# Expert routing lists built on chip and spread over the last mixer block, in one program block instead of four

## The reference, cut to what matters

```
lg  = h2 @ w_rg + b_rg                 # 4 groups, the best one is taken
le  = h2 @ w_re + b_re                 # 32 experts, top 2 of the 8 in that group
gate = softmax(top 2) * softmax(lg)[group]
# each (token, expert) pair is given a slot in a block that one expert owns
hid = silu(x[block] @ w_gate[e]) * (x[block] @ w_up[e])
y[token] += (hid @ w_down[e]) * gate
out = rmsnorm(x + y, g_final)
```

## Time and profile before

| | us |
|---|---|
| median of 3 runs (1652.87 to 1655.18) | 1653.35 |
| profiled execution: its own time | 1655.35 |
| profiled execution: span, first to last instruction | 1653.70 |
| PE busy | 1497.3 (91%) |
| DVE busy | 1035.1 (63%) |
| ACT busy | 867.5 (52%) |
| POOL busy | 340.5 (21%) |

### The profile page before, as it was taken

The page is one execution under the profiler, slowest core; times in us unless marked ns, Lnnn a source line. Parts: engine busy times, 40 slices in busy tenths (PEclk is TensorE's granted clock), DMA queues, the critical chain, the costliest instruction groups (busy, mean ns, idle before and its releaser), DMA issues. The chain is left out here.

```text
span 1653.7 us, 24203 instructions
## 1 busy us (share of the span) xinstructions
PE 1497.3 (91%) x8174; PEld 1250.7 (76%) x8174; DVE 1035.1 (63%) x1491; ACT 867.5 (52%) x1177; POOL 340.5 (21%) x486
## 2 busy tenths in 40 slices
PE   6999999999999999999999606999999999999980
PEld 5888899988889998888999604767666666666650
DVE  4565444656444546654453326899888888888853
ACT  4644433464444336544432214777777777777742
POOL 1122111111111111212110041222222223222213
PEclk9999999999999999999999757999999999999995
DMA  6222533342234435223332138999999999999956
GB/s 226 77 80 95 189 115 117 117 162 77 90 128 153 129 101 179 77 89 116 115 127 96 77 115 319 376 381 371 380 373 378 379 371 380 375 379 378 372 185 238
DMA packets 71504, 350.77 MB, mean 212 GB/s; under 512 B 10705, under 2 KB 10978, under 8 KB 46706
## 3 DMA queue, kind: packets, MB, share of 16 engines
q1 hardware_dynamic: 57554, 310.05, 50.6%
q0 software_dynamic: 9824, 25.28, 6.6%
q10 hardware_dynamic: 4048, 14.42, 2.3%
HBM read 322.42 MB, written 27.75 MB: 212 GB/s over the span
## 5 line engine op out<-in xcount | busy, mean ns | idle before, releaser
L1227 DVE TENSOR_TENSOR wlo<-est,whi 128x2048 fp32r<-128x2048 f32 x193 | 440.9, 2291 | 112.8 <-ACT whi L1223 85.4
L1223 ACT ACTIVATE whi<-est 128x2048 fp32r<-128x2048 f32 x193 | 369.3, 1916 | 151.4 <-DMA est<-wexp 115.9
L734 DVE TENSOR_TENSOR w<-stage,w 128x1024 fp32r<-128x1024 f32 x171 | 219.6, 1311 | 65.9 <-ACT w L483 64.0
L1582 PE MATMUL ps<-whi,xT 128*96 128x512 f32 x512 | 205.3, 401 | 24.7 <-DVE xT L1532 24.4
L483 ACT ACTIVATE w<-stage 128x1024 fp32r<-128x1024 f32 x171 | 174.3, 1052 | 101.2 <-PE ps L995 86.5
L1584 PE MATMUL ps<-whi,xT 128*96 128x512 f32 x512 | 203.3, 397 | 0.0
L1583 PE MATMUL ps<-wlo,xT 128*96 128x512 f32 x512 | 202.4, 395 | 0.0
L993 PE MATMUL ps<-w,hT 128*128 128x384 f32 x576 | 199.8, 347 | 0.0
L995 PE MATMUL ps<-w,hT 128*128 128x384 f32 x576 | 193.5, 336 | 0.0
L994 PE MATMUL ps<-w,hT 128*128 128x384 f32 x576 | 193.3, 336 | 0.0
L993 PE MATMUL ps<-hT,w 128*128 128x384 f32 x408 | 138.2, 339 | 4.7 <-DVE w L734 3.5
(11 more groups left out here) (221 smaller groups left out, 2681.0 us busy)
## 6 DMA issues: line engine op xcount, KB each, us to landing
est<-wexp SPq DMA_DIRECT2D x193, 1024.0 KB, 13.9
stage<-wmix SPq DMA_DIRECT2D x171, 512.0 KB, 3.6
H<-x_all SPq DMA_DIRECT2D x9, 512.0 KB, 8.2
XR<-x_all SPq DMA_DIRECT2D x9, 512.0 KB, 5.2
x_scratch<-XR ACTq DMA_DIRECT2D x9, 512.0 KB, 2.8
h_scratch<-H ACTq DMA_DIRECT2D x9, 512.0 KB, 5.0
cx<-x_scratch SPq DMA_DIRECT2D x9, 512.0 KB, 8.4
y_all<-co ACTq DMA_DIRECT2D x9, 512.0 KB, 6.7
```

Of the source, the lines that this page charges most:

```text
L734: vec.tensor_tensor(whl[w % 2][1][o], stage[r % STAGE][:], whl[w % 2][0][o].bitcast(F32), ALU.subtract).then_inc(w_lo, 1)
L1223: act.activation(whi[q][:], est[q][:], ACT.Copy).then_inc(e_hi[q], 1)
L1227: vec.tensor_tensor(wlo[q][:], est[q][:], whi[q][:].bitcast(F32), ALU.subtract).then_inc(e_lo[q], 1)
L1582: pe.matmul(out, A[0][ka], B[0][kb], start=start, stop=False)
```

## The change

The four program blocks become one, without the engines meeting between them. The list in DRAM goes (with its initial fill, the eighteen writes and all reads). Instead DVE makes, for each of 18 columns of pairs (nine tiles, two choices), a one-hot matrix `R` of the pair's slot within its block and a one-hot row `bk` of its block times the token's number, and PE adds up `R`-transposed times `bk`: the result, 96 slots by 32 experts, is the list. A second set of 18 such products (`bk2`) makes the gates and the lists of further blocks of experts with over 96 pairs. Each expert now always has a first block (block number = expert number), further blocks come behind block 31, and SP's loads ahead of the loop use the block number as the expert's. A slot without a pair gets index 2048; the gather has a bound and no error for it, and the scatter takes the spare row.

Ranking of the first six tiles (`rank_parts(0, 6)`, three parts) moves into the last group's z stage at d = 3, 4, 5; their rank products behind out product 2; their placement and the split of the first two weight pieces between the adds of column groups 1 and 2. Only the last three tiles are ranked behind the last logits. SP issues the last group's stores and, in its own order, loads for blocks 0, 1 and piece (2, 0) before the loop. In the loop POOL copies a column of the on-chip list into a 96x1 index tile twice a block (`gix`, `six`) in place of two list reads; DVE copies the gate column (`gwb`), which ACT's `y_out` waits for. Buffers are laid out anew: the tiles of pieces 0 and 1 lie where hT and oT were.

```diff
             def e_first(b, q):                       # SP, behind the last mixer weights
+                if b:
+                    sp.wait_ge(e_lo[q], b)
+                sp.dma_start(est[q][:], wexp[b, q]).then_inc(e_in[q], 16)
+            sp.wait_ge(br_mm, SUPER * DC)
+            for q in range(2):
+                e_first(0, q)
...
+            for j in range(TPS):
+                sp.wait_ge(n2_h, tot(last, TPS, j + 1))
+                sp.dma_start(h2_dram[...], H[j][:]).then_inc(h2_st[j], 16)
+                sp.dma_start(x2_dram[...], XR[j][:]).then_inc(x2_st[j], 16)
+            sp.wait_ge(out_mm, X2_OUT)
+            for q in (2, 3, 4):
+                e_first(0, q)
+            sp.wait_ge(log_mm, tot(last, TPS, TPS))
+            e_first(0, 5)
+            for b, q in ((1, 0), (1, 1), (1, 2), (1, 3), (2, 0)):
+                e_first(b, q)
+            sp.wait_ge(r_meta, 1)
...
+            hi(0, 0, True)                            # ACT, behind the out stage's splits
+            hi(0, 1, True)
+            square2(0, last)
+            square2(1, last)
+            act.wait_ge(w_lo, SUPER * NP_SB + SEED)
+            evac2(0)
+            square2(2, last)
+            evac2(1)
+            evac2(2)
...
+            def y_out(b):                             # ACT
+                act.wait_ge(e_used[5], b + 1)
+                act.wait_ge(gwb_cp, b + 1)
+                act.wait_ge(y_free, b + SEED)
+                act.activation(yS[:, 0:512], ps[0:TB, 5, :], ACT.Copy, scale=gwb[:]).then_inc(y_act, 1)
...
+            def gather(b, rows, first=False):         # POOL
+                if not first:
+                    pool.wait_ge(gx_tr, b)
+                pool.indirect_dma_start(out=gX[:], out_offset=None, in_=h2_dram,
+                                        in_offset=bass.IndirectOffsetOnAxis(ap=rows, axis=0),
+                                        bounds_check=ROWS - 1, oob_is_err=False).then_inc(gx_in, 16)
+            def gather_of(b):
+                pool.wait_ge(gx_in, b * 16)
+                pool.tensor_copy(gix[:], gidxf[:, bass.ds(b, 1)]).then_inc(gx_cp, 1)
+                pool.wait_ge(gx_cp, b - 2)
+                gather(b, gix[:])
+            def scatter(b):
+                pool.tensor_copy(six[:], sidx[:, bass.ds(b, 1)]).then_inc(six_cp, 1)
...
+            with pool.Fori(0, third_last) as b:
+                gather_of(b + 3)
+                scatter(b)
+                stored(b)
...
+            def place(part_, t0, nt, T):              # DVE
+                vec.wait_ge(r_rmm, part_ + 1)
+                link(vec.tensor_tensor(pick[:], oh[:], ranks..., ALU.mult))
+                link(vec.tensor_reduce(rk[:, i2], pick..., AX.X, ALU.add))
+                link(vec.tensor_tensor(cmp[:], rk..., steps..., ALU.is_ge))
+                link(vec.tensor_reduce(kq[:, i2], cmp[:], AX.X, ALU.add))
+                free(vec.scalar_tensor_tensor(key[:, i2], eid..., float(KEY), kq[:, i2], ALU.mult, ALU.add))
+                link(vec.scalar_tensor_tensor(slot[:, i2], kq[:, i2], -float(TB), rk[:, i2], ALU.mult, ALU.add))
+                free(vec.tensor_tensor(R[:, i2, :], cst3(C_SLOT, TB)..., slot..., ALU.is_equal))
+                link(vec.tensor_tensor(bk[:, i2, :], cst3(C_KEY, EXPERTS)..., key..., ALU.is_equal))
+                vec.tensor_tensor(b4, b4, tok, ALU.mult).then_inc(r_place, 1)
...
+            place(0, 0, EARLY, RA)                    # DVE, behind add_x2(1, 2)
+            lo(0, 0)
+            lo(0, 1)
+            add_x2(2, 0, last)
+            add_x2(2, 1, last)
+            norm2(0, last)
+            add_x2(2, 2, last)
+            norm2(1, last)
+            norm2(2, last)
             for j in range(TPS):
-                add_logits(j, SUPER - 1, j % 2, 0)
+                add_logits(j, last, 1, 0)
+            for _ in rank_parts(EARLY, TPS, RB):
+                pass
+            place(1, EARLY, TPS, RB)
+            vec.wait_ge(r_lmm, 1)
+            vec.tensor_scalar(gidx[:], lists, float(PAD_ROW), None, ALU.add).then_inc(r_list, 1)
...
+            x_lo(0)
+            lo(0, 2)
+            lo(0, 3)
+            pair_gates()
+            lo(1, 0)
+            body(0, first=True)
...
+            def list_mm(i0, i1):                      # PE
+                for i in range(i0, i1):
+                    ins = pe.matmul(ps[0:TB, B_LIST, 0:EXPERTS], R[:, i, :], bk[:, i, :], start=i == 0, stop=i == NP2 - 1)
...
+            route_logits(2, last, h2E[:, 2 * D:3 * D], 1, 0)
+            pe.wait_ge(r_place, 1)
+            list_mm(0, 2 * EARLY)
+            rank_mm(1, EARLY, TPS, RB)
...
+            pe.wait_ge(r_place, 2)
+            list_mm(2 * EARLY, NP2).then_inc(r_lmm, 1)
```

More of the change, by code:

```diff
@@ L234, in build, with fits, piece @@
         scr = mz[:, :, :].rearrange("p a b -> p (a b)")[:, 0:D]
+        def fits(end):
+            assert place[0] <= end, (place[0], end)
+        est, whi, wlo = [None] * EP, [None] * EP, [None] * EP
+        def piece(kind, q):
+            name, tiles = (("est", est), ("whi", whi), ("wlo", wlo))[kind]
+            tiles[q] = at(f"{name}{q}", [P, EPC], F32R if kind else F32)
         place[0] = keep_base
-        est = [at(f"est{i}", [P, EPC]) for i in range(EP)]
-        assert place[0] <= oT_end
+        for q in range(2):
+            for kind in range(3):
+                piece(kind, q)
@@ L240, in build @@
+        fits(oT_end)
         place[0] = oT_end
-        whi = [at(f"whi{i}", [P, EPC], F32R) for i in range(EP)]
-        wlo = [at(f"wlo{i}", [P, EPC], F32R) for i in range(EP)]
+        for kind, q in ((0, 2), (0, 3), (0, 4), (0, 5), (2, 5), (1, 2), (2, 2), (1, 3), (2, 3), (1, 4), (2, 4), (1, 5)):
+            piece(kind, q)
+        fits(xr_at)
+        place[0] = xr_at
         gX = at("gX", [TB, D])
         xT = [at(f"xT{i}", [P, DC, TB], F32R) for i in range(2)]
+        hid = at("hid", [TB, DE])
@@ L274, in build @@
[L274 to L281, removed]
+        gate = at("gate", [P, TILES, 2])
+        gsum, pg, dd, ex, den, g1 = (at(n, [P, TILES]) for n in ("gsum", "pg", "dd", "ex", "den", "g1"))
         cntc = at("cntc", [EXPERTS, 1])
-        cmp = at("cmp", [EXPERTS, MAX_PER_EXPERT])
@@ L630, in _, with hi, evac2 @@
                     square2(2, s)
-            last = SUPER - 1
-            for j in range(TPS):
-                square2(j, last)
-            for j in range(TPS):
+            def hi(b, q, first=False):
+                act.wait_ge(e_in[q], b * 16 + 16)
+                if not first:
+                    act.wait_ge(e_used[q], b)
+                act.activation(whi[q][:], est[q][:], ACT.Copy).then_inc(e_hi[q], 1)
+            def evac2(j):
                 for g in range(2):
@@ new lines, in _, with store @@
+            act.sem_inc(y_free, SEED)
+            x_hi(0, True)
+            for j in range(TPS):
+                act.wait_ge(h2_st[j], ST_END)
+            hi(1, 0)
+            body(0, first=True)
+            act.wait_ge(r_meta, 1)
+            end = blocks_of(act, 1)
+            with act.Fori(1, end) as b:
+                body(b)
+            body(end, final=True)
+            y_out(end)
+            def store(t):
+                act.wait_ge(c_out, t + 1)
+                act.dma_start(y_all[t], co[t][:]).then_inc(c_st, 16)
@@ L921, in _ @@
                         mt_low(d - 1)
+                    if s == last and d == 2:
+                        link(vec.memset(ones[:], 1.0))
+                        link(vec.memset(metaf[:], 0.0))
+                        for j in range(TPS):
+                            vec.wait_ge(h2_st[j], last * 16 + 16)
+                    if d >= 3:
+                        next(early, None)
                 m_parts(DC - 1)
@@ L939, in _ @@
                         pass
[L940 to L944 removed]
+                    for j in range(TPS):
+                        add_x2(2, j, s)
                     for _ in split_lo(1, s + 1):
@@ new lines, in _ @@
+            x_lo(0)
+            lo(0, 2)
+            lo(0, 3)
+            pair_gates()
+            for j in range(TPS):
+                vec.wait_ge(h2_st[j], ST_END)
+            lo(1, 0)
+            body(0, first=True)
+            vec.wait_ge(r_meta, 1)
+            end = blocks_of(vec, 1)
+            with vec.Fori(1, end) as b:
+                body(b)
+            body(end, final=True)
+            y_out(end)
+            vec.wait_ge(r_in, 16)
+            vec.tensor_scalar(gfin[:], gfin[:], float(D) ** 0.5, None, ALU.mult).then_inc(g_scaled, 1)
@@ L1637, in _ @@
             gate_up(0, True)
+            pe.wait_ge(r_bk2, 1)
+            for i in range(NP2):
+                ins = pe.matmul(ps[0:TB, B_GW, 0:EXPERTS + 2 * MAX_OVER], R[:, i, :], bk2[:, i, :], start=i == 0,
+                                stop=i == NP2 - 1)
+            ins.then_inc(r_gmm, 1)
             x_transposes(1)
```

886 lines of the change are left out of this document (437 added, 449 removed).

## The result

The changed kernel takes **1614.45 us** (median of 4 runs, 1606.55 to 1619.59) against 1654.26 (4 runs): ratio 0.9755, 95% interval 0.9714 to 0.9796. The forecast was 1603.5, with 1590 to 1618 as range. The profiled execution took 1613.94 us with a span of 1612.1, so 41.6 us of span are gone.

A forecast was written before the change was run, and what follows sets the result against it. The prediction took DMA weight loads to bound the expert stage: 41.3 us from an earlier start plus 8.5 from skipped pads make 49.8, span 1653.70 to 1603.9, forecast 1603.5 us, range 1590 to 1618.

The forecast's parts named there:

- Z stage counted as nothing: Last group's z stage: two thirds of the ranking fits DVE's waits; nothing counted, at most 10.8 us without that cover.
- Out stage: Before PE's ninth out product: added DVE work delays the add to 923.8 and the stage's end from 921.49 to 927.0.
- The last third: Routing after the logits: list ready at 954.3, gate_up(0) at 962.3, 41.5 us earlier, gate_up(1) at 984.3, 38.8 earlier.
- Rival (b): Routing's tail is latency, not work: list ready at 972 instead of 954, gain 18 us less, 1621; chance 0.10.
- Bytes of the pads: Expert stage gathers: 864 pad rows of 4 KB are skipped, saving 0.29 us a block, 8.5 us over 176 pieces.
- rival (a): Expert stage gathers: pads are gathered all the same or cost a descriptor each; gain 41.3 us, 1612; chance 0.20.
- Loads bound the end: Expert stage: weight loads set its end; with skipped pads the last ends at 1535.7, 49.8 us earlier.
- What is added in a block: Expert loop: added DVE and POOL copies cost nothing; POOL's 1.1 us of contention against 0.9 given back.
- rival (c): Expert loop: POOL's copy waits for wlo, PE then waits 0.2 to 0.4 us a block; 1609 to 1613; chance 0.08.
- Rival (d): Expert loop: ACT's y_out behind DVE's last wlo adds 2.64 us to PE's 17.94, blocks 20.6, time 1672; chance 0.05.
- What follows the last load stays: Tail after the last weight load: its length stays unchanged, so nothing is gained there.
- DMA share below 0.95 if a chain, not bytes, sets the block: Mid-stage of the experts: a DMA share under 0.95 would show an engine's chain, not bytes, setting the block.

The follow-up runs named there:

- the four experiments: Pads gathered: changed kernel 1616.0 against 1614.5, POOL's loop turned 1598.9 against 1598.8; pads not scattered: loop turned 1596.6 against 1598.8, index copy early 1594.3 against 1595.6.
- the early index copy: Changed kernel with POOL's index copy for the next gather made while the scatter is on its way, the gather still waiting for its landing: 1595.6 us, ratio 0.962.
- opening that ring: POOL's next gather issued before the scatter's landing (1598.8), gate column copied before DVE's last two wlo, its wait for POOL's report moved behind them: 1595.3 us.
- the early gate copy: Kernel with POOL's next gather issued before the scatter's landing (1598.8), DVE's gate column copied ahead of the last two wlo: 1599.2, 1666.4, 1686.9, 1704.2 us.

## Why the prediction held and where it failed

It held in direction and in its range; its value was 11 us too low. That the time lies in the range is partly luck: without 7.9 us that came from a place where it counted on nothing, it would have been 1622, above the range. Its steps:

- **What bounds the kernel before: right.** Half the bytes took the block from 18.57 to 17.66.
- **Z stage counted as nothing: right** to 2.1 us; the second column group's last add runs at 915.25 and `place` begins at 915.72, where 913.6 was forecast.
- **Out stage: mechanism right, size short.** The third group's first add came at 924.58 (forecast 923.8), the wait before the ninth product is 4.08 us, but the out stage's end moved to 929.4, not 927.0, since the first fifteen products behind the wait run at 0.21 us each in place of 0.12 (granted clock 0.61 on the mean of 925 to 929.4, and 1.00 up to the wait). The logits made it up, which is luck: two of three took 1.87, not 3.60, at a granted clock of 1.00 (929.4 to 937.5), and the last add came at 940.45 (forecast 942.4).
- **The last third: right.** Gather 952.7 (954.3), gate_up(0) 960.3 (962.3), gate_up(1) 981.35 (984.3). Rival (b) is out.
- **Bytes of the pads: mis-sized.** The rows are skipped, but 0.29 us a block is not what a skip gives: in the four experiments nothing beyond the spread of the runs shows where 9 us were counted. Of rival (a), "gathered all the same" is false; a packet each they do cost; and that its 1612 is near the time is luck, since it has loads as the bound.
- **"Loads bound the end": the step that failed.** They would have: with the early index copy, where loads do hold the later blocks, the last silu starts 50.8 us earlier than before, and the forecast had 49.8. (That is no proof of its terms: the blocks there are 18.04 and then 18.43, not 18.34, and 8.5 of the 49.8 are the pads.) But the changed kernel's own limit lies above it, at 18.88 us a block.
- **What is added in a block, "nothing": wrong, and this is rival (c).** The comparison was 1.1 us of contention against 0.9 given back. One copy in this trace took 2.84, and the gather behind it 5.26 rather than 1.01: the prediction charged the copy for its wait and forgot that the DMA issue behind it is an instruction of POOL too, 0.97 us at the median before and 2.72 after. It also took its 2.1 us to spare from one block, where PE already waited for gathers in others. Over the 18.04 of a block with its gather in time, the mean block has 0.84 us more, 26 in all; (c) had 0.2 to 0.4. The Trainium skill's GPSIMD Engine Reference (Key points) says that POOL shares its SBUF interfaces with VectorE and contends with DVE instructions of two SBUF inputs, and the trace agrees: of POOL's gathers those beside wlo took up to 5.26 us, those beside small wlo 1.04 at most.
- **Rival (d), ACT's y_out behind wlo: there, but small.** It sets 18.04 where PE alone needs 17.66, 0.38 us and not 2.64 (of which 0.35 for copy and wait, with no row named, is 0.25 in the rows above). It sets the short blocks, but opening that ring gained nothing beyond the runs' spread: 1595.3 against 1598.8, since loads come next.
- **"What follows the last load stays": wrong by 7.9 us** to the good. 5.9 of it is the barrier ahead of the last reads. The prediction priced a barrier at 0.6 us at most, at each of three places; at this one it was 6. The other 2.0 were not followed up.
- **The sign "DMA share below 0.95 if a chain, not bytes, sets the block": wrong.** A chain set it at 1.01. The wait of ACT for pieces and the pieces' landing time were the signs; and so was the prediction's own "gX landing well before the transposes, else (c)".

Put together: the forecast's account has the last silu at 1588.0 - 49.8 = 1538.2; it is at 1554.25, 16.0 later, and the tail is 7.9 shorter. That is 8.2 us more than the forecast span of 1603.9, the 1612.1 of the profiled execution.

Every version that frees the gather beats both kernels, but for the one with the early gate copy; among those that compute the same result, the index copy made early (1595.6) and, not told apart from it, the same with the scatter skipping pads (1594.3), 0.962 and 0.963 of the kernel before, are lowest. Weight loads hold both in their later blocks, at 18.4 us a block.

## What to carry to other kernels

Where several limits lie within 7% of each other (here 17.66, 18.04, 18.4, 18.88), price each chain of a block by itself, and with it the issuing instructions of its transfers. On a serial chain of landings, move off everything that does not need the landing; here a copy that takes 0.18 us undisturbed was worth 19 us. To tell whether transfers bind, read who waits for them, not how busy they are.

## What the runs showed of the hardware

- A POOL instruction beside DVE's weight split can wait for more than one DVE instruction: a scatter's issue took 10.27 us in place of 1.45, a gather's 5.26 in place of 1.01, a 96x1 cast 4.57 in place of 0.18; with the split cut to 128 columns no gather took over 1.04. It is not always the whole run: in the rows shown the index copies end where a wlo ends (1109.46, 1226.00, 1236.92), but the one at 1232.35 sat through the border between two wlos, and the one at 1223.39 got through at such a border. What decides at a border is not shown. Making DVE busier (the early gate copy) can so make POOL's transfers later.
- A DMA share of 1.01 stood beside a landing time of 7.6 us and no waits for pieces in one kernel, and 1.02 beside 13.9 us and 87.4 us of waits in the other.
- 3.5 MB fewer bytes of skipped rows, in as many packets, gave no more than the runs' spread, though the time of that queue's packets fell from 5.9% to 4.8% of the 16 engines' span.
